# Mix loop of a transformer kernel: where the softmax scaling, the gate and the sums of squares run

## The reference, cut to what matters

```python
a  = mla_mixer(...)      # 4 heads, causal softmax over 512 keys, 4 query blocks of 128
gm = u * (einsum('hts,bcshd->bcthd', w, rms_norm(v)) + b_spatial)        # the gate
po = (windowed means - pin) @ w_pool * pool_scale                         # the pool
mix = concatenate([rms_norm(a), rms_norm(gm), rms_norm(po)])
x  = x + mix @ w_out
# softmax of one block: p = exp(scale * s - max), then p / sum(p), then p @ v
```

## Time and profile before

| | |
|---|---|
| median of three runs | 2698.09 us (2691.52 to 2700.82) |
| the profiled execution | 2697.78 us, span 2695.9 us |
| TensorE busy | 2607.8 us, 97% |
| VectorE busy | 1173.2 us, 44% |
| ScalarE busy | 501.1 us, 19% |
| GpSimd busy | 1626.1 us, 60% |
| mean granted TensorE clock | 0.985 |
| layer 0 mix loop | about 102 to 159 us |
| layer 1 mix loop | about 654 to 710 us |

### The profile page before, as it was taken

One profiled execution on the slowest core, in us unless ns is written; L12 is line 12 of the kernel. 1 busy time (PEld: TensorE's weight loads), 2 busy tenths in 40 slices (PEclk: granted clock), 3 DMA queues, 4 the chain that ended last, 5 costly groups with the idle time before them and its releaser, 6 DMA issues.

```text
span 2695.9 us, 31577 instructions
## 1 busy us (share of the span) xinstructions
PE 2607.8 (97%) x11906; PEld 2142.7 (79%) x11906; DVE 1173.2 (44%) x1678; ACT 501.1 (19%) x849; POOL 1626.1 (60%) x1113
## 2 busy tenths in 40 slices
PE   7889999999899999999999999999999999999997
PEld 6768888888578888887888888888788878888885
DVE  5754443036644440345540513783467155504325
ACT  3342111023421110201200103200310044100022
POOL 5526667664266676666676766676246615767763
PEclk9999999999899999999999999999999999999998
DMA  4102222231022222222232223222112202222221
GB/s 153 63 16 94 97 105 94 93 115 63 16 94 98 104 93 94 94 94 94 102 106 97 93 94 104 93 98 104 48 47 100 103 32 73 94 106 94 94 93 63
DMA packets 36892, 236.71 MB, mean 88 GB/s; under 512 B 4048, under 2 KB 5584, under 8 KB 9168
## 3 DMA queue, kind: packets, MB, share of 16 engines
q1 hardware_dynamic: 33456, 230.78, 24.6%
q10 hardware_dynamic: 3360, 4.85, 0.6%
HBM read 233.51 MB, written 2.10 MB: 87 GB/s over the span
## 4 chain that ended last, share of the span: by engine, by line
PE 93%; DVE 4%; ACT 1%; issue 1%; POOL 0%; DMA 0%; DVEq 0%; SPq 0%; POOLq 0%; ACTq 0%
PE psum L469 29%; PE psum L470 28%; PE psum L471 28%; PE psum L918 2%; PE psum L902 1%; PE psum L680 1%; PE psum L927 1%; PE psum L790 1%; PE psum L806 0%; DVE work L1335 0%; PE psum L499 0%; DMA x_res<-in_x 0%; POOL w_low L411 0%; PE psum L752 0%; DVE stat L1676 0%
## 5 line engine op out<-in xcount | busy, mean ns | idle before, releaser
L411 POOL TENSOR_TENSOR w_low<-w_stage,w_high 128x512 fp32r<-128x512 f32 x864 | 1178.7, 1395 | 18.0
L407 POOL TENSOR_SCALAR w_high<-w_stage 128x2048 fp32r<-128x2048 f32 x216 | 416.3, 1928 | 1014.8 <-PE psum L471 1003.5
L469 PE MATMUL psum<-x_high,w_high 128*128 128x512 f32 x1664 | 654.2, 393 | 17.0 <-DVE x_low L1351 17.0
L470 PE MATMUL psum<-x_low,w_high 128*128 128x512 f32 x1664 | 649.3, 390 | 0.0
L471 PE MATMUL psum<-x_high,w_low 128*128 128x512 f32 x1664 | 649.0, 390 | 0.0
L469 PEld LDWEIGHTS psum<-x_high,w_high 128*128 128x128 f32 x1664 | 313.4, 188 | 85.1 <-issue 17.1
L470 PEld LDWEIGHTS psum<-x_low,w_high 128*128 128x128 f32 x1664 | 313.3, 188 | 67.0 <-issue 2.2
L471 PEld LDWEIGHTS psum<-x_high,w_low 128*128 128x128 f32 x1664 | 313.3, 188 | 65.2
L469 PE MATMUL psum<-mlp_high,w_high 128*128 (+1 forms) x576 | 224.3, 389 | 2.8 <-DVE mlp_low L1468 2.8
L1392 DVE TENSOR_TENSOR psum<-psum,x_res 128x512 f32<-128x512 f32 x56 | 39.2, 700 | 426.8 <-PE psum L471 423.8
L471 PE MATMUL psum<-mlp_high,w_low 128*128 (+1 forms) x576 | 224.2, 389 | 0.0
(11 more groups left out here) (266 smaller groups left out, 3486.2 us busy)
## 6 DMA issues: line engine op xcount, KB each, us to landing
w_stage<-in_wstream SPq DMA_DIRECT2D x216, 1024.0 KB, 4.9
x_res<-in_x SPq DMA_DIRECT2D x2, 1024.0 KB, 11.7
out_x<-attn_out SPq DMA_DIRECT2D x8, 256.0 KB, 2.1
inv_count_sb<-in_inv_count ACTq DMA_DIRECT2D x2, 512.0 KB, 9.0
ple_proj<-in_p ACTq DMA_DIRECT2D x2, 512.0 KB, 3.7
qk<-in_mask ACTq DMA_DIRECT2D x1, 576.0 KB, 3.8
w_spat<-in_spatial ACTq DMA_DIRECT2D x2, 256.0 KB, 5.5
diag_sb<-in_diag ACTq DMA_DIRECT2D x2, 256.0 KB, 9.7
```

Source lines behind the costliest of these rows:

```text
L407: pool.tensor_scalar(wh[:, s, :], stage[:, s, :], 1.0, 1.0, ALU.mult, ALU.mult).then_inc(high_written, 1)
L411: last = pool.tensor_tensor(wl[:, s, part], stage[:, s, part], wh[:, s, part].bitcast(F32), ALU.subtract)
L469: pe.matmul(out, wa, ra, start=start, stop=False)
L470: pe.matmul(out, wa, rb, start=False, stop=False)
```

## The change

Four edits, all in the mix phase:

1. The scaling of the probabilities by 1/sum moves from VectorE (L1685) to ScalarE. VectorE still takes the reciprocal and signals `sum_inverted`; ScalarE does the scaling of step t-1 between the exponential of step t and the copy of step t-2.
2. The gate adds its bias in place in PSUM and multiplies from there; the PSUM bank is released after the multiplication and no longer after the addition.
3. The squares of the gate and of the pool are no longer added on VectorE. TensorE reads both tiles and sums them in PSUM: eight matmuls of one column where there were four, at the same steps 13 and 15. The reader of the squares' slots is now TensorE's sum.
4. The maximum is negated and scaled by `tensor_scalar` with a pointer, in place of `scalar_tensor_tensor`.

```diff
+            def sum_of_squares(p, b, first):
+
+                take(p, b)
+                sums[1] += 1
+                pe.wait_ge(squares_ready, p.squares + first + 2)
+                for c in range(TOK):
+                    for n in range(2):
+                        last = pe.matmul(ps[:, b, c:c + 1], W[:, SQ[n], c * P:(c + 1) * P], ones[:, 0:1], start=n == 0, stop=n == 1)
+                last.then_inc(summed, 1)
...
-                           13: lambda: token_sum(p, 2, 2), 15: lambda: token_sum(p, 3, 2)}
+                           13: lambda: sum_of_squares(p, 2, DT), 15: lambda: sum_of_squares(p, 3, DT + 2)}
...
+                def squares_to_pe(at, src):
+                    n = square(src)
+                    reader[n % 2] = (summed, state["sums"] + at + 1)
...
-                    square_tiles([u[:, 0, :], u[:, 1, :]])
+                    for f in range(2):
+                        squares_to_pe(0, u[:, f, :])
...
-                        square_tiles([po[:, f, :]])
+                        squares_to_pe(1, po[:, f, :])
...
+                    if 1 <= t <= steps:
+                        q = t - 1
+                        n = (q % TOK + 1) * P
+                        act.wait_ge(sum_inverted, L * steps + q + 1)
+                        act.activation(W[:, q % 3, 0:n], W[:, q % 3, 0:n], ACT.Copy, scale=stat[:, 22 + q % 2:23 + q % 2]) \
+                            .then_inc(probs_ready, 1)
...
-                    tt(W[:, RSH, :].rearrange("p (c q) -> p c q", q=P), ps[:, 2 + f, :].rearrange("p (c q) -> p c q", q=P),
-                       bsp[:, f:f + 1, :].to_broadcast([P, TOK, P]), ALU.add).then_inc(drained[2 + f], 1)
-                    dve.wait_ge(drained[2 + f], d[2 + f] + 5)
-                    tt(u[:, f, :], u[:, f, :], W[:, RSH, :], ALU.mult).then_inc(gate_ready, 1)
+                    z = ps[:, 2 + f, :].rearrange("p (c q) -> p c q", q=P)
+                    step(tt(z, z, bsp[:, f:f + 1, :].to_broadcast([P, TOK, P]), ALU.add))
+                    tt(u[:, f, :], ps[:, 2 + f, :], u[:, f, :], ALU.mult).then_inc(gate_ready, 1)
                     dve.wait_ge(gate_ready, 2 * L + f + 1)
+                    dve.sem_inc(drained[2 + f], 1)
-
-                def gate_sum():
-                    accumulate(True)
-                    accumulate(False)
...
-                def pool_sum():
-                    accumulate(True)
-                    accumulate(False)
...
-                        dve.scalar_tensor_tensor(out=stat[:, t % 3:t % 3 + 1], in0=mx, scalar=-1.0, in1=nar[:, 184 + t:185 + t],
-                                                 op0=ALU.mult, op1=ALU.mult).then_inc(max_ready, 1)
+                        dve.tensor_scalar(stat[:, t % 3:t % 3 + 1], mx, nar[:, 184 + t:185 + t], -1.0, ALU.mult, ALU.mult) \
+                            .then_inc(max_ready, 1)
...
-                        step(dve.reciprocal(stat[:, 22 + q % 2:23 + q % 2], stat[:, 3 + q % 3:4 + q % 3]))
-                        dve.tensor_scalar(W[:, q % 3, 0:n], W[:, q % 3, 0:n], stat[:, 22 + q % 2:23 + q % 2], None, ALU.mult) \
-                            .then_inc(probs_ready, 1)
+                        dve.reciprocal(stat[:, 22 + q % 2:23 + q % 2], stat[:, 3 + q % 3:4 + q % 3]).then_inc(sum_inverted, 1)
```

More of the change, by code:

```diff
@@ L274, in build @@
         gate_scaled = sem("gate_scaled")
+        sum_inverted = sem("sum_inverted")
         squares_ready = sem("squares_ready")
@@ L1618, in gate @@
                     dve.wait_ge(z_done, L * 4 + f + 1)
-                    tt(W[:, RSH, :].rearrange("p (c q) -> p c q", q=P), ps[:, 2 + f, :].rearrange("p (c q) -> p c q", q=P),
-                       bsp[:, f:f + 1, :].to_broadcast([P, TOK, P]), ALU.add).then_inc(drained[2 + f], 1)
-                    dve.wait_ge(drained[2 + f], d[2 + f] + 5)
-                    tt(u[:, f, :], u[:, f, :], W[:, RSH, :], ALU.mult).then_inc(gate_ready, 1)
+                    z = ps[:, 2 + f, :].rearrange("p (c q) -> p c q", q=P)
+                    step(tt(z, z, bsp[:, f:f + 1, :].to_broadcast([P, TOK, P]), ALU.add))
+                    tt(u[:, f, :], ps[:, 2 + f, :], u[:, f, :], ALU.mult).then_inc(gate_ready, 1)
                     dve.wait_ge(gate_ready, 2 * L + f + 1)
-                def gate_sum():
-                    accumulate(True)
-                    accumulate(False)
-                    state["acc_sum"] = state["sums"] + 1
-                def pool_sum():
-                    accumulate(True)
-                    accumulate(False)
-                    state["acc_sum"] = state["sums"] + 2
+                    dve.sem_inc(drained[2 + f], 1)
                 def repeat_norm(b, count):
@@ L1660, in low_out @@
                         tt(mix_low[k], tile, mix_high[k].bitcast(F32), ALU.subtract).then_inc(split_low, 1)
-                between = {2: lambda: pool_input(0), 3: lambda: pool_input(1), 6: lambda: gate(0), 7: lambda: gate(1), 9: gate_sum, 14: pool_sum}
+                between = {2: lambda: pool_input(0), 3: lambda: pool_input(1), 6: lambda: gate(0), 7: lambda: gate(1)}
                 steps = HEADS * TOK
@@ L1681, in mix @@
                         q = t - 1
-                        n = (q % TOK + 1) * P
                         dve.wait_ge(exp_ready, L * steps + q + 1)
-                        step(dve.reciprocal(stat[:, 22 + q % 2:23 + q % 2], stat[:, 3 + q % 3:4 + q % 3]))
-                        dve.tensor_scalar(W[:, q % 3, 0:n], W[:, q % 3, 0:n], stat[:, 22 + q % 2:23 + q % 2], None, ALU.mult) \
-                            .then_inc(probs_ready, 1)
+                        dve.reciprocal(stat[:, 22 + q % 2:23 + q % 2], stat[:, 3 + q % 3:4 + q % 3]).then_inc(sum_inverted, 1)
                 state["scaled"] = DT * L
+                state["sq"] += 4
                 repeat_norm(2, d[2] + 7)
                 repeat_norm(3, d[3] + 7)
-                state["acc_sum"] = state["sums"]
                 for h in range(HEADS - 1):
```

## The result

The changed kernel takes 2711.95 us (median of five runs, 2707.1 to 2713.02) against 2698.09 us before (2691.52 to 2703.84): 1.0045 times, with a 95% interval of 1.0034 to 1.0056. It is slower by 12 us by the ratio and 14 by the medians; the interval allows 9 to 15. The profiled execution took 2713.0 us, with a span of 2711.2 us.

A forecast was written before the change was run, and what follows sets the result against it. TensorE was taken as the bound, for 93% of the span. Layers of -2.1 and -1.7 us gave -3.8, with +0.8 for the clock -3.0: 2697.8 to 2694.8, plus 0.3 for the median, 2695.1 us; range 2686 to 2704.

The forecast's parts named there:

- the term for TensorE's clock: Mix loops: half a chance of a fall before the pool, half of 2.2 us back; together +0.8 us.
- The layout at full clock: First half: each engine's instructions in order with estimated durations; pool's products end at 138.0 us in layer 0, 690.3 in layer 1.
- The four waits of TensorE: First half: 2.1 us at step 2, 2.9 at step 8, 1.1 at step 9, 1.7 before head 1's values.
- GpSimd's end: Pool's products, step 11: GpSimd's window sums leave only 4.0 and 3.4 us of room, whatever becomes of VectorE.
- VectorE's half: First half, layer 0: VectorE busy 21.25 of 23.6 us; the change takes 13.5 away, so it no longer bounds.
- The sum of 3.6 us per layer: Second half, pool's products to table load: moved scalings, a new wait and slower maxima make it 3.6 us later.
- ScalarE's wait for the sum: Second half: the pool's first square waits for TensorE's doubled sum of the gate's squares at step 13, 1.7 us.
- The clock in the second half: Second half: at full clock all through, 1.7 and 0.5 us come back, 2.2 together, at half a chance.
- -5.7 + 3.6 and -5.3 + 3.6: Layers 0 and 1: first half earlier plus second half later, giving -2.1 and -1.7 us.
- The second rival: Mix loops: TensorE's clock falls to 0.50 in the first half and stays there to the table load; 2707.2 us, chance 0.09.
- Passing on one to one: Behind the loop: the loop's change reaches the total whole, since the next slab's split waits for TensorE to release its slot.
- the third rival: Mix loops: ScalarE becomes the bound, scaling gains little in first half, costs 3.6 us per layer; 2699.3 us, chance 0.17.

The follow-up runs named there:

- Scaling only: Kernel before with only the probabilities' scaling moved from VectorE to ScalarE: 2709.95 us, 1.0041 times before.
- gate and maximum: Kernel before with only the gate's in-place bias and multiplication in PSUM and the maximum's pointer form: 2692.36 us, 0.9970 times before.
- the spare slots: Changed kernel with the pool's squares written to two free tiles, so ScalarE doesn't wait for TensorE's sum: 2707.00 us, 1.0031 times before.
- squares only: Kernel before with only the squares of gate and pool summed by TensorE instead of added on VectorE: 2707.09 us, 1.0027 times before.
- second profile: Profile of the changed kernel run once more, with nothing altered: 2708.85 us, 1.0037 times before.

## Why the prediction was wrong

The step that failed is the term for TensorE's clock, priced at +0.8 us over both layers. It came to 10.5 and 12.3 us in the two profiles of the changed kernel, in the first halves and in the second. Without it the sum was right within 1 us.

- **The first half, as a chain.** The layout at full clock was right: 23.6 us from the split to the products' end, 24.0 measured. The four waits of TensorE in it were 2.1, 2.9, 1.1 and 1.7 us, and came as 2.04, 2.88, 0.85 and 0.46 in layer 0 of the changed kernel. That GpSimd's end is the floor was right too. The changed kernel took 26.1 and 27.8, then 27.8 and 27.9: 2.1 to 3.9 us more than 24.0. The values before the products ran at about half the clock in both layers of both profiles (4.48 to 4.64 us for 2.42). In the three longer halves the clock also fell a first time, before the transposes of step 6, which came at 15.8 us for 14.2. I had taken +1.5 us per layer for such a fall, at half a chance.
- **What bounds the first half.** VectorE's 21.25 busy of 23.6 us was read as "VectorE's half", and all its work as relief. Not all of it was. Scaling only took 8.1 us of work away and the half was as long as before, after a lead of 3.1 and 1.9 us that ScalarE's queue and the clock used up; the maxima and the gate took 6.1 away and gave 4.0 and 3.5. Busy time said who worked, not what the relief would be worth at the next meeting of two engines.
- **Two readings of the rows.** The prediction has L1673 and the gate's addition untouched by GpSimd because they read one operand from SBUF. L1685 reads one as well, besides its pointer, and took 1.39 for 0.49. And six scalings lie between 114.3 and 137.9 us, the longest 1.51, not seven with 1.39; their sum of 6.8 is right.
- **The second half, by its parts.** The sum of 3.6 us per layer was right: 15.60 - 11.87 = 3.7 us, changed kernel against kernel before, both at full clock and with matmuls in step 13. Its largest term, ScalarE's wait for the sum, was 1.7 and came as 1.52 at full clock; it was 2.91 in the changed kernel, where the sum itself ran at half the clock. The scalings were taken at 2.0 and cost 1.9 (14.8 - 12.9, with gate and maximum in both).
- **The clock in the second half.** I had let it give back 2.2 us with half a chance. Before, the second halves lost 1.7 and 0.9 us to the clock (13.54 and 12.78 against 11.87); after, they lose 3.6 in each (19.2 against 15.6), in all four cases. The low stretch lasted 10.2 us where it had lasted 3.4, and held the doubled sum and the values. Why it lasted longer is shown in part only. TensorE's gap ahead of step 13's sum grew from 1.40 to 1.81 us, and that by the scalings ahead of it on ScalarE: it is 1.81 with the spare slots too, which have no wait for the sum, 1.90 and 1.82 with scaling only, and 1.40 with squares only. But the spare slots have a clock of 0.80, and squares only 0.78, so this gap alone doesn't do it. Scaling only has 0.73; each of the edits 1 and 3 lowers the clock by itself, and both together give 0.69.
- **The sum.** -5.7 + 3.6 and -5.3 + 3.6 gave -3.8 without the clock; the loops measured +7.5 and +9.3, 11.3 and 13.1 us above it. Against 24.0 and 15.6 us in each layer the changed kernel lost 13.1 and 14.9 us to the clock, and before had lost 2.6 in the second halves, so the clock explains 10.5 and 12.3 of the miss. 6.4 and 8.2 us of the miss lie in the first halves, 4.9 in the second. The +0.8 was also added up wrongly: 3.0 less 2.2 takes both terms whole, at half a chance each they give +0.4.
- **The second rival.** It had the clock, 2707.2 us and a chance of 0.09, the lowest but one, and came nearest. Its mechanism held in part: the clock fell before the pool and again behind it, but it didn't stay low from the first half to the table load; from 142.2 to 149.0 us it was 1.00. Its sign, a clock under 0.6 in the second half, was too strict: 0.69 was enough. The prediction's own sign of being wrong, a clock that moves by more than 0.1, came true there (0.87 to 0.69).
- **Passing on one to one.** Right: 30.1 and 29.9 us behind the table load, as before.
- **The page of the Trainium skill.** "ScalarE: Activation LUTs", section "Rules for kernel authors", keeps multiplications on VectorE. By the runs it was the better guide here: with the scaling on ScalarE the kernel before became 10.5 us slower. The rule gives the time per element as its reason. Here 512 columns took 0.71 us on ScalarE, as in the earlier trace rows; the trace of scaling only shows the loss of the first half in the queue behind the scaling and in the clock, and 2.7 and 3.4 us more in the second half. By the third rival, to which I had put that rule, it would have been +1.2 us: the sign was right, the price was not.

## What to carry to other kernels

Follow a relief to the next place where two engines meet before counting it. 8.1 us of scalings taken from the busiest engine put TensorE 3.1 us ahead and were lost before the next meeting; 6.1 us of maxima and gate brought 4.0, and with them in place the scalings brought nothing more. Work moved to an in-order engine brings its wait along, and everything ready behind it waits too. Where TensorE has gaps, price a change in them twice, once as it is and once with the work behind it at half the clock. Matmuls that nobody needs, put into a gap, can test this, and can pay. But look at what comes behind: behind the loop, where VectorE set the length of a stretch, a full clock brought nothing there, and the longer gap that it left put the fall on the projection.

## What the runs showed of the hardware

- TensorE's granted clock fell in stretches where TensorE had gaps of 1.4 to 3.8 us, and could stay low while TensorE was busy: in the changed kernel, second profile, it was 0.65, 0.50 and 0.57 in the three stretches of 4 us from 145 to 157 us, with TensorE busy for 3.29, 3.58 and 4.00 us of them. With nine, twelve and eight matmuls in the three gaps it was 1.00 for 39.6 us in one layer, and 0.93 and 0.77 in the halves of the other, in the same execution. The Trainium skill's page "TensorE: Matmul & The Clock Gate", section "Part 1: The HAM clock gate (the "warmup" mystery)", has the two levels and says that the moment of the change to the faster one varies from run to run. The trace agrees that the moments vary, and here falls too come and go: the first half of layer 0 of the changed kernel took 26.07 us at 0.87 in one execution and 27.82 at 0.75 in the other.
- A one-column `tensor_scalar` with a pointer on VectorE takes 0.21 us beside GpSimd and without it, in both phases; the one-column `scalar_tensor_tensor` 0.16 alone and up to 1.03 beside it. GpSimd gains too: its window sums ended 22.3 us behind the split where they had ended 23.5 and 23.8 behind it.
- Sixteen records of one-column sums took 1.84 to 1.95 us at full clock and 3.17 to 3.34 where it fell to half at their start; eight took 0.95 to 1.12.
